# Three page buffers in paged attention, output weights loaded a stage earlier, and one-hop barriers in a two-layer decoder step

## The chip, the core and the metric

The kernel runs on one core of a Trainium2 chip. A core has five engines that run their own instruction streams: PE (matrix products), DVE and ACT (elementwise work), POOL (GpSimd) and SP (which here only issues transfers). Sixteen DMA engines move data between the main memory and the on-chip memory. The engines order their work by semaphores: one waits until a counter has reached a value, another adds to it.

The metric is the device time of one execution in microseconds; lower is better.

## What is computed

A prompt of 512 tokens and 8 samples of 8 new tokens each go through two layers. Layer 0 mixes tokens by softmax attention with a forget bias; the samples attend to 512 past rows each, which lie in four pages of 128 rows that a page table names. Layer 1 is an mLSTM. After each mixer comes a mixture of 32 experts, of which each token takes two.

```python
for layer in range(DEPTH):
    hp = rmsnorm(xp, norm_mix[layer]); hs = rmsnorm(xs, norm_mix[layer])
    if layer % N_MIXERS == 0:
        qp, kp, vp, lfp = fox_project(hp, fox_w_in[j], fox_b_f[j])
        cp = jnp.cumsum(lfp, axis=1)
        op = fox_attention(qp, kp, vp, cp, cp, 0)
        k_past = gather_pages(cache_k[j], page_table)
        v_past = gather_pages(cache_v[j], page_table)
        ...
        xp = xp + fox_output(op, fox_w_out[j])
        xs = xs + fox_output(os_, fox_w_out[j])
    else:
        ...
    # then x = x + hier_moe(rmsnorm(x)): top group, top 2 of its 8 experts,
    # each down(silu(x @ w_gate) * (x @ w_up)), weighted
```

## The kernel before

Everything is in 32-bit floats. The 576 tokens are five row tiles (four of 128 prompt rows, one of 64 sample rows). The program is seven phases: the projection of layer 0 (`fox_project`), its attention (`fox_attention`), its output product and experts (`out_and_experts(0, ...)`), the mLSTM projection, the mLSTM itself, `out_and_experts(1, ...)`, and the final norm with the outputs.
**Projection.** ACT squares each row tile, DVE scales it, PE turns it (L385), DVE puts it into `turned` with the gains (L495). Then PE makes the forget gates (L391) from all 576 tokens, and the keys in eight blocks of 128 columns (L357, `keys`). POOL meanwhile loads the past log-forget rows in a loop of 32 small transfers (L342), which starts when the last of the five square roots (L338) is done. From the fifth key block on PE turns these rows (L366, `turn_past`); it first waits for all 32 (`past_in`). Then come values (L416) and queries (L438). At its end SP fills the buffer `expert_rows` in main memory with nine transfers of 512 KB (`fill_rows`).

**Attention.** First the prompt: 8 pairs of heads, 4 query tiles each, `STEPS` = 32 steps. Per pair SP loads four blocks of forget rows (L235, `tri_rows`), and in the pairs' gaps a page each of sample 0's keys (SP) and values (POOL), both through `load_page` (L548). Then the samples b = 0 to 7, one after the other: PE turns the sample's four key pages (L714, `d_turn_keys`, in two halves), makes scores (L756), turns the weights of the sample before (L725, L726), multiplies them with its value pages (L738), and turns the result (L764). A sample has 2 MB of key pages and 2 MB of value pages. Key pages have two buffers, `kpg` and the memory of the prompt's queries; value pages have two, `vpg` and the memory of the prompt's keys. SP issues the keys of sample b once those of sample b-2 are turned (`kt_done`), POOL the values of b once those of b-2 are multiplied (`do_done`). Both second buffers are free only when the prompt's last scores are made (`s_done` at `STEPS`), so sample 1's pages are issued then.

**Output product and experts.** SP loads the 4 MB of output weights `w` into the memory of the third expert buffer (L1071). PE runs four products with no use (L191, `idle_products`), then the output product (L1175), which DVE adds to the residual rows `x` (`add_tile`). Then routing, and 16 pairs of experts, whose weights (6 MB a pair, L1039, L1047 and L1061) go round three buffers: the next pair's load is issued when PE has finished with the pair three before it. The loads of the third buffer wait for the whole output product.

## Time and profile before

| | us |
|---|---|
| median of 3 runs | 1433.36 |
| lowest and highest | 1431.96, 1446.88 |
| the profiled execution's own time | 1446.13 |
| its span in the trace | 1444.4 |

| engine | busy us | share |
|---|---|---|
| PE | 1258.4 | 87% |
| DVE | 370.4 | 26% |
| ACT | 246.7 | 17% |
| POOL | 214.1 | 15% |

The transfers move 342.60 MB, 237 GB/s over the span. Read these shares with care: they are means over phases that have different limits. For a change in one phase one reads that phase: which engine has gaps there, and what ended them. A matmul row gives the start, the busy time, the line, the tiles and in brackets the idle time ahead of it with what ended it. PEq, POOLq and SPq are the engines' own instruction queues.

### The profile page before, as it was taken

The fourth block names the chain that finished last, engine by engine and source line by source line (L and its number), as shares of the span: only waits on it lengthen the run. The fifth ranks groups of instructions, "written<-read, shape, count | busy, mean of one in ns | idle before, by whom it ended". The sixth has DMA issues, their size and how long they took to land.

```text
span 1444.4 us, 16231 instructions
## 1 busy us (share of the span) xinstructions
PE 1258.4 (87%) x6275; PEld 665.3 (46%) x6275; DVE 370.4 (26%) x792; ACT 246.7 (17%) x571; POOL 214.1 (15%) x268
## 2 busy tenths in 40 slices
PE   6999998889789989988877999999879989988780
PEld 4764575556544533333324764444654543333230
DVE  4131003554310541111115400112620441111115
ACT  2000004653210301000003200013420201000001
POOL 2300002321200011111101000211930011111102
PEclk9999999999989999999998999999979999999995
DMA  8310534749958579999959032212139469999975
GB/s 279 100 44 23 188 132 116 236 151 323 366 190 338 192 262 418 419 420 419 416 231 318 21 110 50 84 47 81 31 137 363 181 212 413 420 419 419 420 297 204
DMA packets 104397, 342.60 MB, mean 237 GB/s; under 512 B 21534, under 2 KB 40162, under 8 KB 80506
## 3 DMA queue, kind: packets, MB, share of 16 engines
q1 hardware_dynamic: 89176, 305.47, 55.5%
q0 software_dynamic: 14848, 35.94, 6.9%
q8 instruction: 54, 0.88, 0.3%
q14 instruction: 29, 0.24, 0.0%
q10 hardware_dynamic: 290, 0.07, 0.0%
HBM read 320.08 MB, written 36.02 MB: 247 GB/s over the span
## 4 chain that ended last, share of the span: by engine, by line
PE 55%; SPq 16%; DMA 12%; DVE 6%; issue 4%; ACT 2%; POOL 2%; POOLq 2%; DVEq 0%; ACTq 0%
SPq L1039 9%; PE ps L1759 8%; PE ps L1175 8%; PE ps L1250 7%; SPq L1061 4%; PE ps L438 4%; DMA moe_gu<-in_moe_w_up 4%; PE ps L416 4%; PE ps L1710 4%; DMA moe_wd<-in_moe_w_down 3%; PE ps L1268 2%; DMA fox_arena<-in_cache_k 2%; PE ps L357 2%; PE ps L696 1%; PE ps L1770 1%
## 5 line engine op out<-in xcount | busy, mean ns | idle before, releaser
L1250 PE MATMUL ps<-moe_gu,rows 128*64 128x512 f32 x1024 | 249.8, 644 | 49.9 <-DMA moe_gu<-in_moe_w_up 47.3
L1250 PEld LDWEIGHTS ps<-moe_gu,rows 128*64 128x64 f32 x1024 | 82.4, 148 | 197.6 <-issue 188.8
L1759 PE MATMUL ps<-mwblk,turned 128*128 128x512 f32 x256 | 111.5, 593 | 2.3 <-DVE vaug L1962 1.5
L1175 PE MATMUL ps<-moe_gu,turned 128*128 128x512 f32 x256 | 110.2, 592 | 0.0
L1537 DVE TENSOR_TENSOR turned<-turned,ps 128x256 f32<-128x256 f32 x32 | 13.5, 421 | 304.8 <-ACT turned L1353 304.8
L1135 POOL DMA_INDIRECT expert_rows<-turned,moe_row x32 | 32.0, 1001 | 390.8 <-ACT turned L1363 358.4
L1268 PE MATMUL ps<-moe_wd,moe_rowsel 128*64 128x512 f32 x352 | 80.4, 598 | 2.8 <-DMA moe_wd<-in_moe_w_down 2.8
L1175 PEld LDWEIGHTS ps<-moe_gu,turned 128*128 128x128 f32 x256 | 48.7, 190 | 61.5 <-issue 61.5
L1759 PEld LDWEIGHTS ps<-mwblk,turned 128*128 128x128 f32 x256 | 48.0, 190 | 61.0 <-issue 57.4
L1353 ACT ACTIVATE turned<-ps 128x256 f32<-128x256 f32 x32 | 12.3, 383 | 301.9 <-PE ps L1250 301.9
L357 PE MATMUL ps<-turned,fox_arena 128*128 128x288 f32 x256 | 63.1, 407 | 0.0
L438 PE MATMUL ps<-turned,fox_arena 128*128 128x288 f32 x256 | 62.3, 407 | 0.0
L416 PE MATMUL ps<-fox_arena,turned 128*128 128x512 f32 x128 | 57.6, 606 | 2.5 <-issue 2.5
L191 PE MATMUL ps<-cst 128*128 128x512 f32 x76 | 46.4, 756 | 13.1 <-POOLq L2506 13.1
L438 PEld LDWEIGHTS ps<-turned,fox_arena 128*128 128x128 f32 x256 | 48.6, 190 | 14.1 <-issue 0.8
L1710 PE MATMUL ps<-turned,mwblk 128*128 128x288 f32 x224 | 54.5, 406 | 0.0
L357 PEld LDWEIGHTS ps<-turned,fox_arena 128*128 128x128 f32 x256 | 48.3, 190 | 13.4 <-issue 0.5
L241 POOL TENSOR_TENSOR fox_arena<-fox_arena,cst 128x256 f32<-128x256 f32 x32 | 23.1, 727 | 205.8 <-DMA fox_arena<-negc_rows 205.6
L1710 PEld LDWEIGHTS ps<-turned,mwblk 128*128 128x128 f32 x224 | 42.6, 190 | 11.7
L873 DVE CUSTOM_DVE_ANT_0 fox_arena<-ps,fox_arena 128x128 f32<-128x128 f32 (+3 forms) x64 | 28.2, 478 | 66.4 <-PE ps L673 66.4
L1128 POOL DMA_INDIRECT turned<-h_rows,moe_row x32 | 33.2, 1036 | 76.6 <-DVE moe_row L1496 43.1
L1542 DVE COPY turned<-ps 128x512 f32<-128x512 f32 x32 | 22.1, 691 | 86.8 <-PE ps L1268 86.8
(345 smaller groups left out, 1522.7 us busy)
## 6 DMA issues: line engine op xcount, KB each, us to landing
moe_gu<-in_moe_w_gate SPq DMA_DIRECT2D x56, 1024.0 KB, 21.8
moe_gu<-in_moe_w_up SPq DMA_DIRECT2D x56, 1024.0 KB, 24.0
moe_wd<-in_moe_w_down SPq DMA_DIRECT2D x44, 1024.0 KB, 24.3
rows<-in_moe_w_down SPq DMA_DIRECT2D x20, 1024.0 KB, 22.3
fox_arena<-in_cache_k SPq DMA_DIRECT2D x32, 512.0 KB, 8.2
fox_arena<-in_cache_v POOLq DMA_DIRECT2D x32, 512.0 KB, 9.5
fox_arena<-in_fox_w_in SPq DMA_DIRECT2D x6, 2048.0 KB, 10.3
mwblk<-in_mlstm_w_in SPq DMA_DIRECT2D x6, 2048.0 KB, 8.6
```

What stands on the lines that cost most here:

```text
L191: pe.matmul(ps[:, bank, :], ident, const("ones")[:, 0:512], start=True, stop=True)
L357: mm = pe.matmul(ps[:, 2 * (g % 3) + half, 0:HT], wblk[:, g // 4, c, (g % 4) * P:(g % 4 + 1) * P], turned[:, c, half * HT:(half + 1) * HT] ...
L416: mm = pe.matmul(ps[:, m % 4, :], turned[:, c, n * P:(n + 1) * P], wblk[:, (2 + blk) % 3, c, :], start=(c == 0), stop=(c == KC - 1))
L438: mm = pe.matmul(ps[:, 2 * ((g + 2) % 4) + half, 0:HT], wblk[:, (4 + g // 4) % 3, c, (g % 4) * P:(g % 4 + 1) * P], turned[:, c, half * HT: ...
L1039: sp.dma_start(gu[p % SLOTS][:, half, k], i[name][layer, 2 * p + half].rearrange("(p c) n -> p c n", c=KC)).then_inc(gu_in[p % SLOTS], 16)
L1061: sp.dma_start(wd[p % SLOTS][:, half], i["moe_w_down"][layer, 2 * p + half].rearrange("(p c) n -> p c n", c=2)).then_inc(down_in[p % SLOTS ...
L1128: pool.indirect_dma_start(xg[:, s, :], None, h_dram[layer], bass.IndirectOffsetOnAxis(ap=rows_of(0, p), axis=0), bounds_check=TOK - 1, oob ...
L1175: mm = pe.matmul(ps[:, 2 * n + half, :], turned[:, c, n * P:(n + 1) * P], w[:, c, half * 512:half * 512 + 512], start=(c == 0), stop=(c == ...
L1250: mm = pe.matmul(ps[h, 2 + p % 2, :].rearrange("s (k f) -> s k f", k=2), xT[:, c, h], gu[s][:, half, :, c, :], start=(c == 0), stop=(c == ...
L1268: mm = pe.matmul(ps[h, 5 + n, :], aT[p % 2][:, m, h], wd[s][:, half, m, n * 512:(n + 1) * 512], start=(m == 0), stop=(m == 1))
L1710: mm = pe.matmul(ps[:, bank + half, 0:HT], wblk[:, k % 3, c, g * P:(g + 1) * P], turned[:, c, half * HT:(half + 1) * HT], start=(c == 0), ...
L1759: mm = pe.matmul(ps[:, m % 4, :], turned[:, c, n * P:(n + 1) * P], wblk[:, k % 3, c, :], start=(c == 0), stop=(c == KC - 1))
```

## The change

1. **Three buffers of pages.** The keys' third buffer is `x[:, 0:4, :]` (the residual rows of the prompt), the values' third is the memory of `sc`. SP loads sample 1's key pages into `x` during the last four pairs of the prompt, sample 2's after the prompt's scores, and from then on sample b+1's when sample b-2's are turned. POOL issues sample 1's values after the prompt's scores, sample 2's after its outputs, then b+1's when b-2's are multiplied. As `x` is overwritten, SP loads the four prompt row tiles again at the end of attention (`x_again`), and DVE waits for them ahead of the first `add_tile`.
2. **Output weights a phase earlier.** SP loads layer 0's output weights during the last samples, into memory that is then free; `multiply_out` of layer 0 no longer runs the four products of `idle_products`.
3. **Barriers.** Every engine, POOL too, drains, adds one to `together`, and waits for all five.
4. **First phase.** Nine products of the identity ahead of the first turning; an activation ahead of the first square; gates and first key block in two halves of 288 tokens, the first after three row tiles; three instead of four PSUM places for turned tiles.
5. The filling of `expert_rows` is gone.
6. Sample 0's first four key turnings stand ahead of the last pair's value product; DVE's first key copy waits for that product.

```diff
@@ -174,14 +174,9 @@
 
 
 
-        filled = lasting("filled")
-
-        def fill_rows(sp):
-
-            for row in range(0, 2 * TOK, P):
-                sp.dma_start(y_dram[row:row + P, :], x[:, 0, :]).then_inc(filled, 16)
-
         back_in = [[lasting(f"back_in{layer}_{n}") for n in range(NT)] for layer in range(2)]
+        w0_in, x_again = [lasting(f"w0_in{c}") for c in range(KC)], lasting("x_again")
+        W0_AT = 2 * 8 * D - SB * NPAGE
         back = []
...
             fox_project(pages, arena, qT, kT, v, tri)
-            fox_attention(part, qT, kT, v, pages)
+            w0 = arena[:, W0_AT:W0_AT + KC * D].rearrange("p (c d) -> p c d", d=D)
+            fox_attention(part, qT, kT, v, pages, w0)
             dx.close()
-            out_and_experts(0, i["fox_w_out"][0])
+            out_and_experts(0, i["fox_w_out"][0], w0)
...
-                fill_rows(sp)
                 sp.wait_ge(kv_out, 96)
-                sp.wait_ge(filled, 16 * (2 * TOK // P))
...
+            def flip(pe, n):
+
+                r = ROWS[n]
+                pe.wait_ge(scaled, n + 1)
+                if n >= 3:
+                    pe.wait_ge(gained, n - 2)
+                for c in range(KC):
+                    mm = pe.transpose(ps2[:, 1 + n % 3, c * P:c * P + r], rows[0:r, n, c:D:KC], ident[0:r, 0:r])
+                mm.then_inc(flipped, 1)
+
+            def gates_half(pe, half):
+
+                for c in range(KC):
+                    mm = pe.matmul(ps[0:FH, 6 + half, 0:HT], wf[:, c, :], turned[:, c, half * HT:(half + 1) * HT],
+                                   start=(c == 0), stop=(c == KC - 1))
+                if half:
+                    mm.then_inc(f_done, 1)
+
+            def first_half(pe, half):
+
+                for c in range(KC):
+                    mm = pe.matmul(ps[:, half, 0:HT], wblk[:, 0, c, 0:P], turned[:, c, half * HT:(half + 1) * HT],
+                                   start=(c == 0), stop=(c == KC - 1))
+                if half:
+                    mm.then_inc(k_done, 1)
...
             def pe_(pe):
                 pe.wait_ge(ident_in, 16)
-                for n, r in enumerate(ROWS):
-                    pe.wait_ge(scaled, n + 1)
-                    if n >= 4:
-                        pe.wait_ge(gained, n - 3)
-                    for c in range(KC):
-                        mm = pe.transpose(ps2[:, n % 4, c * P:c * P + r], rows[0:r, n, c:D:KC], ident[0:r, 0:r])
-                    mm.then_inc(flipped, 1)
+                for _ in range(9):
+                    pe.matmul(ps[:, 0, 0:P], ident, ident, start=True, stop=True)
+                for n in range(4):
+                    flip(pe, n)
                 pe.wait_ge(wf_in, 32)
+                pe.wait_ge(gained, 3)
+                gates_half(pe, 0)
+                flip(pe, L)
+                pe.wait_ge(w_in[0], 16)
+                first_half(pe, 0)
                 pe.wait_ge(gained, NT)
-                for c in range(KC):
-                    for half in range(2):
-                        mm = pe.matmul(ps[0:FH, 6 + half, 0:HT], wf[:, c, :], turned[:, c, half * HT:(half + 1) * HT],
-                                       start=(c == 0), stop=(c == KC - 1))
-                mm.then_inc(f_done, 1)
+                gates_half(pe, 1)
+                first_half(pe, 1)
                 for g in range(PAIRS):
-                    keys(pe, g)
+                    if g:
+                        keys(pe, g)
                     if g == 2:
...
-                act.wait_ge(zeroed, 1)
+                act.wait_ge(zeroed, 2)
+                act.activation(rstd[:, 0:1], ms[:, 0:1], ACT.Square)
...
+                dve.memset(ms[:], 1.0).then_inc(zeroed, 1)
...
-            kpg = [part("kpg"), part("qT", NPAGE * D)]
-            vpg = [part("vpg"), part("kT", NPAGE * D)]
-            kpg = [t.rearrange("p (g n) -> p g n", g=NPAGE) for t in kpg]
-            vpg = [t.rearrange("p (g n) -> p g n", g=NPAGE) for t in vpg]
+            kpg = [part("kpg").rearrange("p (g n) -> p g n", g=NPAGE), x[:, 0:NPAGE, :],
+                   part("qT", NPAGE * D).rearrange("p (g n) -> p g n", g=NPAGE)]
+            vpg = [t.rearrange("p (g n) -> p g n", g=NPAGE)
+                   for t in (part("vpg"), part("kT", NPAGE * D), part("sc", NPAGE * D))]
+            RING = len(kpg)
...
-            later = part("tri")
+            later = part("tri")[:, 6 * PROMPT:]
...
                         past_rows(p - 2 - NPAGE)
-                for b in range(1, SB):
-                    if b == 1:
-                        sp.wait_ge(s_done, STEPS)
-                        sp.wait_ge(dec_own, PREP)
-                    else:
+                    if p >= PAIRS - NPAGE:
+                        load_page(sp, i["cache_k"], kpg[1], pages, 1, p - PAIRS + NPAGE, k_in[1])
+
+                def keys_in(b):
+                    for g in range(NPAGE):
+                        load_page(sp, i["cache_k"], kpg[b % RING], pages, b, g, k_in[b % RING])
+
+                sp.wait_ge(s_done, STEPS)
+                sp.wait_ge(dec_own, PREP)
+                keys_in(2)
+                for b in range(2, SB):
+                    if b + 1 < SB:
                         sp.wait_ge(kt_done, PAIRS * (b - 1))
-                    for g in range(NPAGE):
-                        load_page(sp, i["cache_k"], kpg[b % 2], pages, b, g, k_in[b % 2])
-                    if b >= 2:
-                        past_rows(b)
+                        keys_in(b + 1)
+                    past_rows(b)
+
+                def w_chunk(c):
+                    sp.dma_start(w0[:, c, :], i["fox_w_out"][0][c * P:(c + 1) * P, :]).then_inc(w0_in[c], 16)
+
+                sp.wait_ge(kt_done, PAIRS * (SB - 1))
+                w_chunk(0)
+                w_chunk(1)
+                sp.wait_ge(do_done, SB - 1)
+                for c in range(2, 6):
+                    w_chunk(c)
+                sp.wait_ge(dtopped, SB)
+                w_chunk(6)
+                w_chunk(7)
+                sp.wait_ge(kt_done, PAIRS * SB)
+                for n in range(NT - 1):
+                    sp.dma_start(x[:, n, :], i["x_prompt"][0, n * P:(n + 1) * P, :]).then_inc(x_again, 16)
...
+                def values_in(b):
+                    for g in range(NPAGE):
+                        load_page(pool, i["cache_v"], vpg[b % RING], pages, b, g, v_in[b % RING])
...
                     if b == 1:
                         pool.wait_ge(s_done, STEPS)
-                    if b >= 2:
+                        values_in(1)
+                        pool.wait_ge(o_kept, PAIRS)
+                        values_in(2)
+                    if b >= 2 and b + 1 < SB:
                         pool.wait_ge(do_done, b - 1)
-                    for g in range(NPAGE if b else 0):
-                        load_page(pool, i["cache_v"], vpg[b % 2], pages, b, g, v_in[b % 2])
+                        values_in(b + 1)
...
+                    if s == STEPS + 1:
+                        pe.wait_ge(m_done, 2 * STEPS)
+                        pe.wait_ge(k_in[0], 64)
+                        d_turn_keys(pe, 0, range(0, 4))
                     if s >= 5 and s % QT_ == 1:
                         values(pe, (s - 5) // QT_)
                     if 1 <= s <= STEPS:
                         turn_weights(pe, s - 1)
-                pe.wait_ge(m_done, 2 * STEPS)
                 for b in range(SB + 1):
-                    if b < SB:
-                        pe.wait_ge(k_in[b % 2], 64 * (b // 2 + 1))
+                    if 0 < b < SB:
+                        pe.wait_ge(k_in[b % RING], 64 * (b // RING + 1))
                         d_turn_keys(pe, b, range(0, 4))
...
                     if b and p == 1:
                         dve.wait_ge(ds_done, b)
+                    elif p == 1:
+                        dve.wait_ge(pv_done, PAIRS)
...
-            w_in = [sem(tag + f"w_in{c}") for c in range(KC)]
+            w_in = [sem(tag + f"w_in{c}") for c in range(KC)] if layer else w0_in
...
-                for c in range(KC):
+                for c in range(KC if layer else 0):
                     sp.dma_start(w[:, c, :], w_dram[c * P:(c + 1) * P, :]).then_inc(w_in[c], 16)
...
-                idle_products(pe, 4, 0)
+                if layer:
+                    idle_products(pe, 4, 0)
...
+                if layer == 0:
+                    dve.wait_ge(x_again, 16 * (NT - 1))
...
-                if who == "pool":
-                    eng.wait_ge(together, 4 * (n + 1))
-                    eng.drain().then_inc(cleared, 1)
-                else:
-                    eng.drain().then_inc(together, 1)
-                    if who == "sp" and "late" in phase:
-                        phase["late"](eng)
-                    eng.wait_ge(cleared, n + 1)
-                    alone(eng)
+                eng.drain().then_inc(together, 1)
+                if who == "sp" and "late" in phase:
+                    phase["late"](eng)
+                eng.wait_ge(together, 5 * (n + 1))
+                alone(eng)
```

PE's order at the start of the program: L385 and (after) L362 turn row tiles, L391 and L368 are the gates, L357, L376 and L351 the keys, L401 the identity products. Before:

```order
L385 MATMUL ps<-cst,rows 128x128 x32
L385 MATMUL ps<-cst,rows 128x64 x8
L391 MATMUL ps<-turned,fox_arena 16x288 x16
L357 MATMUL ps<-turned,fox_arena 128x288 x48
L399 MATMUL ps<-cst,fox_arena 128x16 x4
```

After:

```order
L401 MATMUL ps<-cst 128x128 x9
L362 MATMUL ps<-cst,rows 128x128 x32
L368 MATMUL ps<-turned,fox_arena 16x288 x8
L362 MATMUL ps<-cst,rows 128x64 x8
L376 MATMUL ps<-turned,fox_arena 128x288 x8
L368 MATMUL ps<-turned,fox_arena 16x288 x8
L376 MATMUL ps<-turned,fox_arena 128x288 x8
L351 MATMUL ps<-turned,fox_arena 128x288 x32
```

Half of the gates and half of the first key block moved ahead of the rest, and the small tile's turning between them; nothing is left out, nine products are added.

PE's order where the prompt's attention ends and the samples begin: L685 and L737 turn the last weights, L696 and L748 multiply values, L703 and L755 spread the sums, L714 and L766 turn sample 0's keys. Before:

```order
L685 MATMUL ps<-cst,fox_arena 128x128 x18
L696 MATMUL ps<-rows,fox_arena 64x512 x2
L696 MATMUL ps<-rows,fox_arena 64x384 x2
L696 MATMUL ps<-rows,fox_arena 64x256 x2
L696 MATMUL ps<-rows,fox_arena 64x128 x2
L703 MATMUL ps<-cst,pa_inv 64x128 x8
L714 MATMUL ps<-cst,fox_arena 128x128 x32
```

After:

```order
L737 MATMUL ps<-cst,fox_arena 128x128 x18
L766 MATMUL ps<-cst,fox_arena 128x128 x16
L748 MATMUL ps<-rows,fox_arena 64x512 x2
L748 MATMUL ps<-rows,fox_arena 64x384 x2
L748 MATMUL ps<-rows,fox_arena 64x256 x2
L748 MATMUL ps<-rows,fox_arena 64x128 x2
L755 MATMUL ps<-cst,pa_inv 64x128 x8
L766 MATMUL ps<-cst,fox_arena 128x128 x16
```

Sixteen of the 32 key turnings moved ahead of the value product.

SP's order at the end of attention; the last rows of each belong to the next phase. L548 and L570 load key pages, L607 and L631 forget rows of the samples, L1071 and L659 the output weights. Before:

```order
L548 DMA fox_arena<-in_cache_k 128x1024
L607 DMA fox_arena<-negs_rows 128x1x512
L1071 DMA moe_gu<-in_fox_w_out 128x1024 x8
L1073 DMA moe_wr<-in_moe_w_group 128x8x4
L1074 DMA moe_wr<-in_moe_w_router 128x8x32
```

After:

```order
L570 DMA x<-in_cache_k 128x1024
L631 DMA fox_arena<-negs_rows 128x1x512 x2
L659 DMA fox_arena<-in_fox_w_out 128x1024 x8
L672 DMA x<-in_x_prompt 128x1024 x4
L1130 DMA moe_wr<-in_moe_w_group 128x8x4
L1131 DMA moe_wr<-in_moe_w_router 128x8x32
```

Twelve transfers of 512 KB now stand in SP's queue ahead of the barrier, where none stood: the eight of the weights, which came behind it, and four new ones.

## Rows read from the trace of the kernel before

**Rows 1.** The windows by phase: time, busy per engine, granted clock, DMA share, GB/s

```profile
233.00:317.00 84.00, 71.90 (x512) 42.21 (x513) 46.10 (x175) 54.36 (x168) 29.38 (x44) 0.97 0.60 182
317.00:347.00 30.00, 28.85 (x320) 19.81 (x321) 12.94 (x28) 9.81 (x19) 3.40 (x7) 0.94 0.88 308
356.00:373.00 17.00, 12.85 (x156) 7.89 (x146) 6.32 (x16) 3.42 (x7) 5.04 (x10) 0.90 1.03 363
415.00:424.00 9.00, 6.42 (x9) 2.75 (x10) 0.15 (x2) 0.00 (x0) 0.56 (x2) 0.62 0.60 215
424.00:479.00 55.00, 55.00 (x130) 24.16 (x130) 3.97 (x6) 3.51 (x6) 1.10 (x2) 1.00 0.69 273
521.00:704.00 183.00, 161.75 (x726) 62.71 (x722) 29.69 (x38) 15.83 (x38) 23.81 (x24) 0.94 1.00 409
```

**Rows 2.** PE's timeline over the samples: start, busy, line, tiles, idle before

```profile
328.75 1.97 PE L714 MATMUL ps<-cst,fox_arena 128*128 128x128 f32 x16
337.80 1.91 PE L714 MATMUL ps<-cst,fox_arena 128*128 128x128 f32 x16
...
346.80 1.91 PE L714 MATMUL ps<-cst,fox_arena 128*128 128x128 f32 x16
...
353.43 3.46 PE L738 MATMUL ps<-fox_arena 128*32 128x256 f32 x40 [2.07 <-DMA fox_arena<-in_cache_v]
```

**Rows 3.** The same timeline, the later samples and the phase's end

```profile
373.14 3.68 PE L714 MATMUL ps<-cst,fox_arena 128*128 128x128 f32 x16 [4.16 <-DMA fox_arena<-in_cache_k]
...
377.68 2.29 PE L714 MATMUL ps<-cst,fox_arena 128*128 128x128 f32 x16
...
397.00 1.97 PE L714 MATMUL ps<-cst,fox_arena 128*128 128x128 f32 x16 [1.74 <-DMA fox_arena<-in_cache_k]
...
401.54 2.37 PE L738 MATMUL ps<-fox_arena 128*32 128x256 f32 x40
...
409.08 4.05 PE L738 MATMUL ps<-fox_arena 128*32 128x256 f32 x40 [0.69 <-ACT fox_arena L846]
```

**Rows 4.** The transfers' issues between 300 and 420: count, size, time to landing

```profile
fox_arena<-in_cache_k SPq DMA_DIRECT2D x28, 512.0 KB, 10.1
fox_arena<-in_cache_v POOLq DMA_DIRECT2D x28, 512.0 KB, 9.8
...
fox_arena<-negs_rows SPq DMA_DIRECT2D x6, 256.0 KB, 14.3
```

**Rows 5.** The chain that ended last, at the first two barriers: start, us, what

```profile
229.24 0.65 ACT fox_arena L476
...
230.01 2.69 POOLq L2506
```

**Rows 6.** The same chain at the second barrier

```profile
414.22 0.22 DVE turned L936
...
414.77 2.67 POOLq L2506
```

**Rows 7.** The drains of POOL at the barriers: least, median, most, ns

```profile
L2506 POOLq DRAIN  x7: 34/2663/2686, 230.0 to 1443.9; - x7
```

**Rows 8.** PE's timeline at the start of the output product

```profile
417.58 6.26 PE L191 MATMUL ps<-cst 128*128 128x512 f32 x8 [3.41 <-POOLq L2506]
423.69 1.88 PE L1175 MATMUL ps<-moe_gu,turned 128*128 128x512 f32 x4
```

**Rows 9.** The timeline of the first phase's start, all engines

```profile
5.24 1.28 ACT L465 ACT_TABLE_LOAD   x1 [5.24 <-DMA x<-in_x_prompt]
...
15.13 0.15 DVE L485 TENSOR_SCALAR ms<-sq 128x1 f32<-128x1 f32 x1
15.19 1.22 DVE L495 TENSOR_TENSOR turned<-ps,gains 128x1024 f32<-128x1024 f32 x1
...
19.08 9.61 PE L391 MATMUL ps<-turned,fox_arena 128*16 128x288 f32 x32 [0.88 <-DVE turned L495]
...
64.40 0.54 POOL L342 DMA_DIRECT2D fox_arena<-in_cache_logf  x1 [0.98 <-issue]
...
69.36 1.04 PE L366 MATMUL ps<-cst,fox_arena 128*16 128x128 f32 x8 [1.09 <-DMA fox_arena<-in_cache_logf]
```

**Rows 10.** SP's queue at the start of the output phase, first and last issues

```profile
417.54 3.85 SPq L1071 DMA_DIRECT2D moe_gu<-in_fox_w_out  x8
...
422.08 4.26 SPq L1074 DMA_DIRECT2D moe_wr<-in_moe_w_router  x1
...
430.67 0.42 SPq L1039 DMA_DIRECT2D moe_gu<-in_moe_w_gate  x1
...
435.83 1.98 SPq L1061 DMA_DIRECT2D moe_wd<-in_moe_w_down  x2
```

**Rows 11.** Forget rows of the prompt (L235): issue to landing, least, median, most

```profile
DMA to landing us min/median/max: 3.5/4.9/8.6
```

19 lines of the change are left out of this document (10 added, 9 removed).

## The prediction

> **What bounds the kernel now.** I read the windows by phase first [rows 1]. In the expert stage (521 to 704) the DMA share is 1.00 at 409 GB/s: the weights are the limit, and PE waits for them. But this stream is started by PE (each load waits for PE to have finished with a buffer), so if all before it comes earlier, the stage does too. Over the prompt's attention (233 to 317) PE is busy 71.9 of 84 us and the DMA share is 0.60; in the samples (317 on) the share is 0.88 and then 1.03, so the pages are the limit there. Then PE's timeline over the samples: sample 1's first key turning begins at 328.75, sample 2's at 337.80, sample 3's at 346.80, without a wait: about 9.0 us each [rows 2]. Sample 7's begins at 397.00, after waits of 2.07, 4.16 and 1.74 us for pages among others [rows 2, 3]. Six periods took 68.25 us where six of 9.0 are 54.0. Last the chain of waits at the barriers: the last engine of the first phase ends at 229.9 and POOL's drain then takes 2.69 us [rows 5]; at the second, 2.67 us [rows 6].
>
> **Samples with three buffers.** The most it can give is 68.25 - 54.0 = 14.25 us. Is there bandwidth for it? After the prompt's scores (312) the kernel before moves 28 key and 28 value pages [rows 4]. After the change four key pages have come earlier, so 24 + 28 = 52 pages of 0.524 MB are left, 27.3 MB, and six forget rows of 0.26 MB: 28.8 MB. Saturated, this stage moved 363 GB/s (356 to 373) and the experts' 409 [rows 1]; I take 385: 75 us, plus some 2 us of gap because the third value buffer is free only at 322, so the last value page lands at about 389. Without waits sample 7 begins at 328.75 + 54.0 = 382.75, and its value product stands as far behind that as before, 409.08 - 397.00 = 12.1 us [rows 3]: 394.8. That fits. Its keys are tighter. They are issued when sample 4's are turned, about 360, and what stands ahead of them is all but five to eight of the pages: 25 MB, landing at 312 + 65 + 2 = 379 at 385 GB/s, at 383 at 363. So sample 7 waits between nothing and a few us. I take 1.25 us off: **13.0 us**; bounds 9 (363 GB/s, and the output weights in between) and 14.25. Sample 0 itself gains nothing: the key turnings fill 0.8 us of PE's idle time ahead of the last value product, but DVE's copies still start behind that product.
>
> What hides the rest: four more key pages in the last four pairs of the prompt, one a pair, 1.3 us of DMA each at 400 GB/s. Forget rows land in 4.9 us at the median, 8.6 at most [rows 11], and are issued one pair ahead, 84 / 8 = 10.5 us. Some 5 us of slack cover 1.3. Cost: 0. The filling of `expert_rows`, 4.7 MB, lies under the query products of the first phase, whose chain is PE's; its going gives 0. The residual rows (2 MB) come back by about 405 and are wanted at the first `add_tile`, some 50 us later: 0.
>
> **Barriers.** POOL's drain took 2.66 us at the median of seven, 34 ns at least [rows 7]. It is long in the phases in which POOL has issued transfers, short in the other two of the middle. After the change POOL drains when its own work is done. At the first two barriers POOL is done long before (its last row turning's load in the first phase is issued at 64.40 [rows 9]), so the drain is hidden. 2.69 + 2.67, less 0.1 us each for the signal: **5.2 us**, and 0.3 us for a PE that stands still 1 us and not 3.6 ahead of the prompt's first scores. At the third and sixth barrier POOL's scatter is what ends last, so its drain stays, and the next phase's first work waits for transfers issued ahead of it: 0. The fourth and fifth lose one signal each: **0.2 us**.
>
> **Output product.** The four idle products run from 417.58 to 423.69, 6.11 us [rows 8]; they go, as the weights are there. 
>
> **First phase.** The table load of ACT (1.28 us at 5.24) goes ahead of the first row tile's arrival [rows 9], and the first turnings run warm, so DVE's chain is 1.3 us earlier and gets back 0.5 us of waiting: the last mean (15.13) about 1.8 us earlier, the third `keep` (15.19 + 1.22) too. Half the gates start at about 14.7, not 19.08, and without their slow start (9.61 us, where 32 records of this size take 7.85 at the upper clock). PE gains 4.4 + 1.8 = some 6 us of lead. But at the fifth key block it waits for the 32 past rows, 1.09 us even before, until 69.36 [rows 9]. POOL's loop of issues is what decides that, and it starts only 1.8 us earlier, so this point comes at 67.5. PE now stands still there for some 4 to 5 us. After an idle time of 4.16 us the same turnings took 3.68 + 2.29 us at 373, against 1.97 + 1.91 elsewhere [rows 2, 3]: 2.1 us, and 0.6 on those between. So the 1.8 us are paid back. **0 us**; bounds -1 and +1.8. The nine identity products end about when the first tile is scaled.
>
> **The sum.** 13.0 + 5.2 + 0.3 + 0.2 + 3.4 + 0 = 22.1 us. The profiled execution took 1446.13 us, its span 1444.4; it would take 1424.0. It stands 12.8 above the median of the runs, 1433.36; I take the same difference from that: **1411.3**. With all lower bounds (9, 3, -1 us) it is 16.7 us: 1416.7; with all upper ones (14.25, 6.11, 1.8) 27.9: 1405.5.
>
> **Rivals.**
> *The pages stay the limit.* A third buffer adds no bandwidth. If the transfers run at 363 GB/s, as between 356 and 373, and not faster, the samples need 79 us, sample 7 waits 4 to 5 us and PE's clock falls again: the term is 8 to 9, the time 1415.5. For it: the share is 1.03 already [rows 1]. Against it: the rate over saturated stretches reaches 409, and the last keys have over 20 us from issue to use. The Trainium skill ("DMA: Bandwidth & Descriptors", "Issuing engines are not separate DMA queues") states that transfers of all engines share the same 16 DMA engines; the keys on SP and the values on POOL then slow one another, as the 14.3 us landing of a 256 KB row [rows 4] shows. Chance 0.20.
> *SP comes late to the barrier.* Twelve transfers stand ahead of its drain. If the queue held no more than some eight, its last issue would wait and the second barrier come 4 us late: 1415. For it: one issue behind the weights took 4.26 us. Against it: from 430.67 SP issued twelve of 1 MB in 7 us [rows 10]. Chance 0.06.
> *The forget rows come late.* The added pages stand ahead of the next pair's rows in SP's queue. It decides from the point where a row takes over 10.5 us less the mask, that is twice its median landing. From there each us goes straight into the last four pairs. At 2 to 4 us a pair 8 to 16 us are lost and the time is within 1% of before (1419 to 1427): chance 0.11. At the price of a whole landing more a pair, 8.6 us, 34 us are lost and it is 1446, slower than before; this needs rows at 17 us. Chance 0.03. Against both: the pairs 2 to 5 carry the same kind of page today and keep their period.
>
> **Chances and range.** Forecast 0.60 (1405 to 1417), pages 0.20, SP 0.06, rows 0.14. A measurement of this kernel can tell about 1%, 14.3 us, from no change: faster means under 1419. Nearly all of the first three is faster; the rows' cases are not, and the runs of before spread over 15 us, which could cost the verdict. Faster 0.84, same 0.12, slower 0.04. Range 1403 to 1420.
>
> **What would show it.** The first gates start near 14.7, but the turning of past rows near 67.5 after a wait of 4 us or more. The prompt's attention starts within 0.5 us of ACT's last copy. Pairs keep 10.4 us. Samples 1 to 7 start 9.0 us apart, the last near 380 on the new time axis (about 3 us less than here); a wait of some us on key pages ahead of sample 6 or 7 is the first rival. The output product starts within 0.5 us of attention's end and runs its first 4 us or so at 1.2 GHz. The expert stage takes what it took, only earlier. I am wrong if the weights' stream gives time back, if pairs 4 to 7 lengthen, or if SP's drain ends behind DVE's.

## The result and the profile after

Three comparisons of the changed kernel were made, each beside runs of the kernel before. The first is the one the prediction is measured by; the two others were made later, with more runs. Experiments were made on different chips, so they are compared by their ratio to the kernel before.

| comparison | changed, us (median, lowest to highest) | before, us (median) | ratio and 95% interval |
|---|---|---|---|
| first | 1423.15 (1417.14 to 1428.57, 4 runs) | 1436.47 | 0.9889 [0.9852, 0.9925] |
| second | 1417.81 (1416.92 to 1421.56, 5 runs) | 1438.82 | 0.9862 [0.9842, 0.9882] |
| third | 1421.01 (1416.40 to 1426.12, 6 runs) | 1439.32 | 0.9876 [0.9841, 0.9912] |
| forecast | 1411.3 (1403 to 1420) | 1433.36 | 0.9846, worked out |

The kernel is faster by 1.1% to 1.4%, on average of the three ratios by 1.24%, 17.9 us of 1438. The forecast was 22.1 us. The direction was right and the median of the first comparison lies 3 us above the range. Of the 11.8 us between 1411.3 and 1423.15 some are of the base: 1433.36 was the median of three runs, and in the later comparisons the kernel before took 1437.9 to 1441.25. In the first comparison the gain was 13.3 us, 8.8 less than forecast; over all three it was 17.9, 4 us less, and behind it stand terms that were off in both directions by more than that.

The profiled execution of the changed kernel took 1428.57 us (span 1426.7, before 1444.4), the longest of its four; that of the kernel before, 1446.13 us, was long for its kernel too. Four places of its trace tell most. First PE's timeline over the later samples, the rows that answer to [rows 2, 3]: start, busy, line, tiles, and in brackets the idle time before and its releaser. L766 turns keys, L777 turns the softmax's weights, L790 is the value product.

```profile
348.75 1.91 PE L766 MATMUL ps<-cst,x 128*128 128x128 f32 x16
...
359.12 1.97 PE L766 MATMUL ps<-cst,fox_arena 128*128 128x128 f32 x16 [1.22 <-DMA fox_arena<-in_cache_k]
363.23 0.66 PE L777 MATMUL ps<-cst,fox_arena 128*128 128x128 f32 x4 [2.14 <-ACT fox_arena L894]
...
372.86 1.97 PE L766 MATMUL ps<-cst,fox_arena 128*128 128x128 f32 x16 [2.51 <-DMA fox_arena<-in_cache_k]
376.92 0.66 PE L777 MATMUL ps<-cst,fox_arena 128*128 128x128 f32 x4 [2.10 <-ACT fox_arena L894]
...
386.87 1.97 PE L766 MATMUL ps<-cst,x 128*128 128x128 f32 x16 [2.83 <-DMA x<-in_cache_k]
391.21 0.66 PE L777 MATMUL ps<-cst,fox_arena 128*128 128x128 f32 x4 [2.38 <-ACT fox_arena L894]
...
402.83 3.83 PE L790 MATMUL ps<-fox_arena 128*32 128x256 f32 x40 [0.69 <-ACT fox_arena L901]
407.27 0.44 PE L816 MATMUL ps<-cst,fox_arena 128*128 128x128 f32 x2 [0.62 <-DVE fox_arena L985]
408.42 1.96 PE L1233 MATMUL ps<-fox_arena,turned 128*128 128x512 f32 x4 [0.70 <-DVEq L2564]
```

Sample 1 begins at 321.71 and samples 1 to 4 stand 9.0 us apart, but samples 5, 6 and 7 wait for key pages, and each then waits a second time in L777, for a softmax whose maximum waited for the forget row. Sample 7 begins 65.2 us behind sample 1; the forecast was 68.25 - 13.0 = 55.25, in the kernel before it was 68.25. And the last value product stands 81.1 us behind sample 1, against 80.3 before: in this profile the stage gained nothing.

Second, the maximum's wait for the forget rows in the same samples, and the rows' time from issue to landing in us (14.3 at the median before [rows 4]):

```profile
L631 SPq DMA_DIRECT2D fox_arena<-negs_rows x6: 535/564/721, 323.2 to 376.0; - x6
...
  DVE fox_arena L967: 19.2, 3
...
DMA to landing us min/median/max: 11.2/18.0/27.0
```

Third, what the DMA queues carried between the first page issue and sample 7's start (q1 is SP's with keys and rows, q0 POOL's with values: packets, MB, share):

```profile
DMA packets 8250, 28.72 MB, mean 354 GB/s; under 512 B 899, under 2 KB 899, under 8 KB 8240
...
q1 hardware_dynamic: 4308, 14.23, 50.1%
q0 software_dynamic: 3932, 14.35, 49.1%
```

All keys and rows that sample 7 needs are 24 pages and six rows, 14.2 MB, and q1 has just carried them. But q0 has carried as much, nearly all 14.7 MB of the values, and the last 2.1 MB of those are wanted only 16 us later. The transfers were busy throughout, partly with bytes that weren't due. How the two queues share the engines shows best where both have work all the time, here from 372 to 382:

```profile
q0 software_dynamic: 544, 1.99, 53.6%
q1 hardware_dynamic: 544, 1.85, 49.5%
```

The packets are equal, the bytes are not. In the three stretches of 10 us before this one the counts are 538 and 539, 527 and 526, 536 and 535; two more profiles of the same kernel differ by 21 packets at most in these stretches. Before 342, with one queue or the other out of work at times, they are not equal. A forget row of 256 KB is 144 packets, as many as a page of 512 KB: where they have a queue of their own, below, six rows are 864 packets and five pages 720.

Fourth, the start of the prompt's attention, behind the barrier of [rows 5]. Before, PE stood idle for 3.65 us, and the value products of the first pair (L696) began 11.35 us behind the scores:

```profile
232.84 3.05 PE L673 MATMUL ps<-fox_arena 64*128 64x128 f32 x12 [3.65 <-POOLq L2506]
...
244.19 2.38 PE L696 MATMUL ps<-rows,fox_arena 128*64 128x512 f32 x16
```

After, the idle time is 0.87 us, and they (L748) begin 9.29 us behind the scores:

```profile
228.69 0.93 PE L725 MATMUL ps<-fox_arena 64*128 64x128 f32 x8 [0.87 <-ACTq L2564]
...
237.98 2.38 PE L748 MATMUL ps<-rows,fox_arena 128*64 128x512 f32 x16
```

In the windows (granted clock third from the end) this stretch has a clock of 1.00; the second row is the output product, which ran at the full clock from its first record and took 55.2 us:

```profile
228.60:238.00 9.40, 7.92 (x50) 4.30 (x50) 5.93 (x26) 8.14 (x25) 2.77 (x4) 1.00 0.64 201
...
408.40:463.60 55.20, 55.18 (x130) 24.31 (x132) 3.95 (x7) 3.30 (x6) 1.45 (x4) 1.00 0.67 267
```

The same stretch in the kernel before had 0.75:

```profile
232.80:244.20 11.40, 10.12 (x50) 5.11 (x50) 5.91 (x26) 8.48 (x25) 3.37 (x5) 0.75 0.82 189
```

The output product begins 1.15 us behind the start of the attention's last product, 408.42 - 407.27. Before, the last product began at 413.74, and the output product 9.95 us behind it, at 423.69 [rows 8]:

```profile
413.74 0.44 PE L764 MATMUL ps<-cst,fox_arena 128*128 128x128 f32 x2 [0.61 <-DVE fox_arena L928]
```

In the changed kernel the clock is back at 1.00 between the last value product and the output product. In the kernel before it had come back too (0.82 in the mean: 1.00 until 415.5, 0.50 from 416.5 on), and it fell again while PE stood idle for 3.41 us at the barrier:

```profile
406.70:408.40 1.70, 0.44 (x2) 0.21 (x3) 0.93 (x3) 0.00 (x0) 0.00 (x0) 1.00 1.03 424
```

```profile
413.20:417.50 4.30, 0.44 (x2) 0.20 (x2) 0.93 (x3) 0.00 (x0) 0.00 (x0) 0.82 0.00 0
417.50:423.70 6.20, 6.12 (x9) 2.58 (x10) 0.15 (x2) 0.00 (x0) 0.56 (x2) 0.57 0.83 293
```

Everything behind the output product came earlier by what had been gained until there (the last phase ends 17.7 us earlier).

### The profile page after: what moved, and what is told of

Its sections match the earlier page's. It is cut to its first block, busy times and chain, and to the rows that moved or that the text cites. A ratio compares the mean times of both kernels' runs of the same rounds, so it can differ in the third digit from the quotient of the medians.

```text
span 1426.7 us, 16246 instructions
## 1 busy us (share of the span) xinstructions
PE 1237.4 (87%) x6285; PEld 654.8 (46%) x6285; DVE 370.4 (26%) x793; ACT 246.7 (17%) x572; POOL 214.4 (15%) x268
## 4 chain that ended last, share of the span: by engine, by line
PE 54%; SPq 16%; DMA 12%; DVE 7%; issue 4%; POOL 3%; ACT 2%; POOLq 2%; DVEq 0%; ACTq 0%
SPq L1096 10%; PE ps L1819 8%; PE ps L1233 8%; PE ps L1308 7%; PE ps L458 4%; DMA moe_gu<-in_moe_w_up 4%; SPq L1118 4%; PE ps L436 4%; PE ps L1770 4%; DMA fox_arena<-negs_rows 3%; PE ps L1326 3%; PE ps L351 2%; DMA moe_wd<-in_moe_w_down 1%; PE ps L748 1%; PE ps L1830 1%
## 5 line engine op out<-in xcount | busy, mean ns | idle before, releaser
L1308 PE MATMUL ps<-moe_gu,rows 128*64 128x512 f32 x1024 | 243.6, 630 | 57.1 <-DMA moe_gu<-in_moe_w_up 53.8
L458 PE MATMUL ps<-turned,fox_arena 128*128 128x288 f32 x256 | 62.3, 406 | 0.0
L436 PE MATMUL ps<-fox_arena,turned 128*128 128x512 f32 x128 | 59.0, 619 | 2.9 <-issue 2.9
L1233 PE MATMUL ps<-fox_arena,turned 128*128 128x512 f32 x128 | 55.2, 593 | 0.7 <-DVEq L2564 0.7
L351 PE MATMUL ps<-turned,fox_arena 128*128 128x288 f32 x224 | 55.2, 406 | 0.0
L1233 PE MATMUL ps<-moe_gu,turned 128*128 128x512 f32 x128 | 55.2, 593 | 0.0
L458 PEld LDWEIGHTS ps<-turned,fox_arena 128*128 128x128 f32 x256 | 48.6, 190 | 14.1 <-issue 0.8
L186 PE MATMUL ps<-cst 128*128 128x512 f32 x68 | 40.0, 731 | 9.5 <-POOLq L2564 8.3
L1770 PEld LDWEIGHTS ps<-turned,mwblk 128*128 128x128 f32 x224 | 42.6, 190 | 11.8
L351 PEld LDWEIGHTS ps<-turned,fox_arena 128*128 128x128 f32 x224 | 42.2, 190 | 11.4
L1600 DVE COPY turned<-ps 128x512 f32<-128x512 f32 x32 | 22.1, 691 | 88.0 <-PE ps L1326 88.0
```

The costliest lines, as they stand in the source:

```text
L186: pe.matmul(ps[:, bank, :], ident, const("ones")[:, 0:512], start=True, stop=True)
L351: mm = pe.matmul(ps[:, 2 * (g % 3) + half, 0:HT], wblk[:, g // 4, c, (g % 4) * P:(g % 4 + 1) * P], turned[:, c, half * HT:(half + 1) * HT] ...
L436: mm = pe.matmul(ps[:, m % 4, :], turned[:, c, n * P:(n + 1) * P], wblk[:, (2 + blk) % 3, c, :], start=(c == 0), stop=(c == KC - 1))
L458: mm = pe.matmul(ps[:, 2 * ((g + 2) % 4) + half, 0:HT], wblk[:, (4 + g // 4) % 3, c, (g % 4) * P:(g % 4 + 1) * P], turned[:, c, half * HT: ...
L1233: mm = pe.matmul(ps[:, 2 * n + half, :], turned[:, c, n * P:(n + 1) * P], w[:, c, half * 512:half * 512 + 512], start=(c == 0), stop=(c == ...
L1308: mm = pe.matmul(ps[h, 2 + p % 2, :].rearrange("s (k f) -> s k f", k=2), xT[:, c, h], gu[s][:, half, :, c, :], start=(c == 0), stop=(c == ...
```

## The experiments

Theory: the third buffer's bytes are there, but they land in the wrong order, since SP's queue (keys, rows) and POOL's queue (values) advance alike. The rival is that the bytes alone are the limit, which no order mends. A second question was how much the barriers gave.

To compare the samples in different profiles I use one interval: from POOL's first value page to the first record of the output phase on PE. It doesn't depend on when the attention began. Where the old barrier stands in it, its 2.7 us are taken off. It is called the **stage** below: 102.3 us before (312.54 to 417.58, less 2.7) and 102.1 in the changed kernel's first profile (306.32 to 408.42).

**Two buffers instead of three**, the rest as changed: from sample 2 on a sample's pages are sent for when those of the sample two before have been read.

```diff
-            kpg = [part("kpg")..., x[:, 0:NPAGE, :], part("qT", NPAGE * D)...]
-            vpg = [... (part("vpg"), part("kT", NPAGE * D), part("sc", NPAGE * D))]
+            kpg = [part("kpg")..., x[:, 0:NPAGE, :]]
+            vpg = [... (part("vpg"), part("kT", NPAGE * D))]
```

> The changed kernel with two buffers of pages in place of three: keys and values of a sample are sent for when the sample before last has been read, as before the change; all else of the change stays. Theory A (the order of landing: keys with rows on SP's queue and values on the software queue are served alike, so values land 12 to 17 us early and what is needed first lands last; the third buffer brought nothing): within 2 us of the changed kernel's profile (the last value product of the samples at 405 to 409 us, the changed kernel has 407.3). Rival B (the third buffer did pay, and something else of the change lost what was expected): 8 to 13 us longer, the last value product at 415 to 420 us.

Measured: 1426.45 us, 0.9908 [0.9878, 0.9938], stage 102.8. As the theory had it: no difference to the first comparison of the changed kernel, 0.9889, that could be told. The 407.3 in the expectation is the start of the attention's last product; it begins at 406.4 here, and the last value product at 403.4, in the changed kernel at 402.8. This was not the last word (below).

**The forget rows by ScalarE.** SP's loop no longer calls `past_rows(b)`; ACT issues them behind its exponentials:

```diff
                     act.activation(pr[:, b % 2, :], ..., ACT.Exp, ...).then_inc(dp_ready, 1)
+                    if b + 2 < SB:
+                        act.dma_start(dbias[:, b % 2, 0:PAST], negs_dram[:, b + 2, :]...).then_inc(db_in[b % 2], 16)
```

> The changed kernel with the forget rows of samples 2 to 7 sent for by ScalarE's own queue, right behind the exponentials of the sample two before, in place of standing behind four key pages on SP's queue. Theory A: the three waits of the maximum's turn (2.14, 2.10 and 2.38 us of TensorE's idle time at samples 2 to 5, with DVE waiting 5.4 to 7.2 us for the rows) go; the waits for key pages (1.22, 2.51, 2.83 us) stay or grow, since the bytes are the same; 2 to 6 us shorter. Rival B (the rows only share the wait with the pages: the bytes are the limit): the key waits grow by what the row waits lose, under 1 us. Rival C: rows land no sooner on the other queue, no change at all in the waits.

Measured: 1414.45 us, 0.9829 [0.9774, 0.9885], stage 93.6. The time is 6.7 us under the changed kernel's mean ratio of 0.9876, more than expected, with an interval of 8 us on either side. The rows land in 8.3 us, nobody waits for them, and of the key waits one is left. In PE's timeline (L765 turns keys, L789 is the value product):

```profile
358.30 1.91 PE L765 MATMUL ps<-cst,fox_arena 128*128 128x128 f32 x16
...
367.30 1.91 PE L765 MATMUL ps<-cst,fox_arena 128*128 128x128 f32 x16
...
378.11 1.97 PE L765 MATMUL ps<-cst,x 128*128 128x128 f32 x16 [1.66 <-DMA x<-in_cache_k]
...
390.20 4.05 PE L789 MATMUL ps<-fox_arena 128*32 128x256 f32 x40 [0.69 <-ACT fox_arena L903]
```

Sample 7 begins 76.2 us behind the first page issue of 301.9, 4.8 less than the 81.1 of the changed kernel. The key waits did not grow; that part of the expectation was wrong, and the queues say why. This is the same kernel, profiled again, from its first page issue to just past sample 7's start:

```profile
q1 hardware_dynamic: 3617, 13.20, 46.5%
q0 software_dynamic: 3358, 12.26, 43.6%
q10 hardware_dynamic: 864, 1.57, 6.5%
```

The rows' 1.57 MB travel on q10. When SP's queue is through with the keys, POOL's has carried 12.26 MB and not 14.35. Sample 7 can begin 2 MB earlier, 5 to 6 us at 354 GB/s. By packets, 864 of the 4320 that sample 7 needs have left SP's queue.

**The values by SP**, on one queue with keys and rows in order of need (`keys_in(b + 1)`, `past_rows(b)`, then the four value pages of b + 1).

> The changed kernel with the value pages of samples 1 to 7 issued by SP, on the same queue as keys and rows, in the order of need: keys of b+1, rows of b, values of b+1. Theory A (two queues served alike bring values 12 to 17 us too early): the waits at samples 4 to 7 shrink, sample 7 begins at 379 to 381 us in place of 386.9, and the kernel is 5 to 8 us shorter than the changed one. Rival B (the bytes by then are the limit, or one queue moves less than two): sample 7 begins at 385 us or later, within 2 us of the changed kernel or longer.

Measured: 1418.30 us, 0.9847 [0.9792, 0.9901], stage 96.6 (from SP's first page issue). Against the changed kernel's mean ratio this is 4 us shorter, which lies within its interval, and the wait for keys at sample 5 is gone. That fits an order that matters, but doesn't show it by itself: sample 7 begins at 384.4, some 4 us later than expected and near the rival's 385. SP waits for a product here before it may issue the next pages, and from the first issue to sample 7 the mean rate was 340 GB/s against 354.

**Half of the value pages.** This kernel leaves out two of each sample's four value pages and multiplies the other two twice, so its result isn't the reference's.

```diff
-                    for g in range(NPAGE):
+                    for g in range(2):
                         load_page(pool, i["cache_v"], vpg[b % RING], ...)
-                        src = vpg[b % RING][:, k, :] if k < NPAGE else ...
+                        src = vpg[b % RING][:, k % 2, :] if k < NPAGE else ...
```

> The changed kernel with two value pages per sample loaded in place of four (the value product reads the two twice, so this part of the computation isn't the reference's): 7.3 MB fewer over the samples' stage, all instructions of the engines the same. If transfers are what holds the samples apart, all six waits go, samples are 9.0 us apart from the first to the last (sample 7 begins 54 to 55 us after sample 1, 65.2 in the changed kernel) and the kernel is 9 to 12 us shorter. If something else holds them (SP's issue, the rows' chain), sample 7 begins 60 us or more after sample 1 and the kernel is under 5 us shorter.

Measured: 1410.33 us, 0.979 [0.9735, 0.9844], stage 90.1. Samples stand 9.0 us apart from the first to the last, sample 7 54.0 us behind sample 1, no wait for pages left. This is what the stage takes when no page is late: the changed kernel's stage is 12 us above it in its first profile, the one with ScalarE's rows 3.5 us.

**The barriers alone**, put into the kernel before (the change's last hunk and nothing else).

> The kernel before with the new barriers alone (every engine signals and waits for five signals). Theory: POOL's drain (2.67 us behind its software transfers) then runs beside the others' drains in place of behind them; the first two barriers give 2.6 us each and the later ones, whose drain is 0.03 us, under 0.2 us: 5.2 us shorter, 0.9964 of before, and a barrier's wait of 0.9 us in place of 3.65 ahead of the prompt's first scores. The prompt's first pair, 11.35 us in the kernel before with a clock of 0.75, then starts warm and gives 2 us more. Rival: POOL's drain ends last anyway, no gain.

Measured: 1425.78 us, 0.9927 [0.9907, 0.9946]: 10.5 us, twice what was forecast. PE's timeline (L191 are the idle products, L1175 is the output product):

```profile
227.77 0.93 PE L673 MATMUL ps<-fox_arena 64*128 64x128 f32 x8 [0.87 <-ACTq L2504]
...
237.06 2.38 PE L696 MATMUL ps<-rows,fox_arena 128*64 128x512 f32 x16
...
410.46 3.67 PE L191 MATMUL ps<-cst 128*128 128x512 f32 x8 [0.70 <-DVEq L2504]
414.27 55.20 PE L1175 MATMUL ps<-moe_gu,turned 128*128 128x512 f32 x128
```

I read four differences against the profile before: the wait at the first barrier 0.87 and not 3.65 (2.8), the prompt's first pair 9.29 and not 11.35 us (2.1), the second wait 0.70 and not 3.41 (2.7), the idle products 3.81 and not 6.11 us from their start to the next product (2.3) [rows 8]. Together 9.9. The barrier's wait was paid twice: PE stood still for 3.65 and 3.41 us, and part of what followed ran at the lower level (0.75 over the first pair, 0.57 over the idle products). Behind 0.87 and 0.70 us of idle time both have 1.00.

**Two buffers and ScalarE's rows**: the first two experiments together.

> Two buffers of pages (as in the first experiment) and the forget rows sent for by ScalarE (as in the second), the rest as changed. The last value product of the samples begins at 390.2 us with three buffers and ScalarE's rows, at 402.8 with three and SP's rows, at 403.4 with two and SP's rows. Theory A (both are needed: the third buffer's bytes are worth what was forecast, once the rows no longer stand behind four pages): the last value product begins 5 to 12 us later than with three buffers and ScalarE's rows, at 395 to 402 us. Rival B (the late rows were all, and the third buffer is worth nothing): at 389 to 393 us, the kernel as short as with three.

Measured: 1426.54 us, 0.9928 [0.9904, 0.9952], stage 102.0, last value product at 401.0: theory A. The rows' place is worth nothing that can be told without the third buffer, which with it is worth 8 to 9 us (102.0 against 93.6). One thing doesn't fit: this kernel has all of the change but the third buffer, and on the same chip it takes no less than the kernel before with the barriers alone (1425.78), though the output product's part should be in it.

**The rows ahead of the keys**, both on SP's queue (`past_rows(b)` moved ahead of the wait for `kt_done` and `keys_in(b + 1)`).

> The changed kernel with the forget rows of sample b still on SP's queue, but ahead of the four key pages of sample b+1 in place of behind them (issued from about 323, 332, ... us on). Theory A (what costs is that rows stand behind 2.1 MB of pages): rows land in 5 to 12 us in place of 18, before they are wanted, no wait of the maximum for them; the last value product begins within 3 us of that with ScalarE's rows (390.2). Rival B (a queue of its own is what helps, since queues are served alike): the rows are in time but the keys land late, the last value product at 396 to 403 us.

Measured: 1428.83 us, 0.9928 [0.9905, 0.9951], stage 106.9, last value product at 406.5: the worst of all with three buffers. The rows take 14.7 us at the median and nobody waits for them, but four waits for key pages add up to 10.4 us. SP's queue shows what was lost. `past_rows(2)` waits for a maximum, so key pages of sample 3, which the changed kernel issues at once behind those of sample 2, left only at 327.5:

```profile
304.79 4.30 SPq L570 DMA_DIRECT2D fox_arena<-in_cache_k  x4
326.14 0.56 SPq L631 DMA_DIRECT2D fox_arena<-negs_rows  x1
327.46 3.67 SPq L570 DMA_DIRECT2D fox_arena<-in_cache_k  x4
```

Rows in time and keys late is rival B's picture, but later than its 396 to 403 us, and the late issue would do the same. So this run did not separate its theories; it shows instead what an order on a queue costs when its head waits.

**The idle products kept.**

```diff
-                if layer:
-                    idle_products(pe, 4, 0)
+                idle_products(pe, 4, 0)
```

> The changed kernel with the four idle products ahead of the first output product kept. The prediction held that leaving them out costs 2.7 us of clock at the start of the output product. Theory A (TensorE goes from the samples' last products into the output product at 1.00 of clock, nothing is lost cold): 3.5 us longer at full clock (four products of 512 columns in f32, 0.87 us each), 6.1 us if they run at half the clock, and the output product no shorter than 55.17 us less 0.3. Rival B (it does run cold without them): the product 2 to 3 us shorter, the kernel 0.5 to 4 us longer.

Measured: 1424.25 us, 0.9902 [0.9864, 0.9940], against 0.9876 of the changed kernel in the mean: some 3.7 us longer, with intervals that overlap. The trace shows theory A: the idle products took 404.72 to 408.22, 3.5 us, and the output product 55.10 us.

**The old barriers in the changed kernel.**

> The changed kernel with the barriers of the kernel before, all else changed. The new barriers alone gave 10.5 us (7.8 to 13.4) against the forecast 5.2. Theory A (a barrier costs twice: its own 2.7 us of serial drain, and a TensorE clock of half that follows the idle 3.4 to 3.7 us, 2.1 us in the prompt's first pair and 2 to 3 us in what follows the second barrier): 8 to 11 us longer than the changed kernel, the output product's first 6 us at a clock under 0.9 and the product 57 to 58 us in place of 55.2. Rival B (only the drains): 5.2 us longer, the product still 55.2 us.

Measured: 1428.61 us, 0.9916 [0.9885, 0.9948]: 5.7 us above the changed kernel's mean (1.3 to 10.4 by this run's interval), less than the 8 to 11 expected. By the time alone that is rival B's number. The trace has theory A's pieces, though:

```profile
228.24 3.06 PE L725 MATMUL ps<-fox_arena 64*128 64x128 f32 x12 [3.65 <-POOLq L2566]
...
239.89 2.37 PE L748 MATMUL ps<-rows,fox_arena 128*64 128x512 f32 x16
...
406.03 58.13 PE L1233 MATMUL ps<-fox_arena,turned 128*128 128x512 f32 x128 [3.40 <-POOLq L2566]
```

Its window of 6 us at the start of the output product:

```profile
406.00:412.00 6.00, 5.97 (x7) 2.53 (x8) 0.15 (x2) 0.00 (x0) 0.55 (x2) 0.50 0.93 280
```

The waits of 3.65 and 3.40 are back, the first pair takes 11.65 us, and the output product 58.13 us, 3.0 more, with a clock of 0.50 in its first 6 us. These make 10.8 us. The stage was shorter here (95.1 us), which gave part of it back in this profile; whether that is chance or a consequence of the later start stays open, and with it what the barriers are worth in the changed kernel.

**The fourth key page by ScalarE**, from sample 3 on; the rows stay on SP's queue.

```diff
-                    for g in range(NPAGE):
+                    for g in range(NPAGE if b == 2 else NPAGE - 1):
                         load_page(sp, i["cache_k"], kpg[b % RING], pages, b, g, k_in[b % RING])
...
                     if b < SB:
                         d_keep_keys(b, 0)
+                    if 1 <= b < SB - 2:
+                        load_page(act, i["cache_k"], kpg[(b + 2) % RING], pages, b + 2, NPAGE - 1, k_in[(b + 2) % RING])
```

> The changed kernel with the last key page of samples 3 to 7 issued by ScalarE's queue (2.6 MB), the forget rows still on SP's queue, now behind three pages. Theory A (queues with work are served alike, and sample 7 begins when SP's queue has carried all its keys and rows; the other queue has carried as much by then): SP's queue carries 11.6 MB in place of 14.2, sample 7 begins 4 to 9 us earlier after the first page issue than the 81.1 us of the changed kernel, at 72 to 77 us, with less than 28 MB moved by then (28.7 in the changed kernel). Rival B (it is the lateness of the rows alone, by its waits in the maximum): sample 7 begins 79 us or more after the first page issue.

Measured: 1416.08 us, 0.9837 [0.9820, 0.9853], stage 93.3: theory A, 0.7 us outside its span of 72 to 77. No wait for pages is left; sample 7 begins at 382.46, 77.7 us behind the first issue, with 26.84 MB carried. Transfers no longer set this time: all samples stand 9.0 to 9.9 us apart. Most stand 9.6 apart and not 9.0, because ACT issues the page ahead of its exponentials, for which PE then waits in L777. ACT's timeline, and then the queues up to sample 7's start:

```profile
335.77 0.60 ACT L890 ACTIVATE rows<-ps 128x512 f32<-128x512 f32 x1 [4.78 <-PE ps L766]
336.45 0.35 ACTq L570 DMA_DIRECT2D x<-in_cache_k  x1
336.85 0.77 ACT L894 ACTIVATE fox_arena<-fox_arena,dnegtop 128x576 f32<-128x576 f32 x1 [0.48 <-issue]
```

```profile
q0 software_dynamic: 3441, 12.56, 44.9%
q1 hardware_dynamic: 3590, 11.53, 41.6%
q10 hardware_dynamic: 720, 2.62, 9.3%
```

No single queue has more than 12.6 MB here. ScalarE's has 720 packets for 2.62 MB, against 864 for the rows' 1.57 MB: in packets the two repairs move about as much.

**The old first phase in the changed kernel** (order of the gates, table load and idle products as before).

> The changed kernel with the first phase's order of the kernel before (no idle products ahead of the turning, no early table load, all gates behind all tokens). By the profiles the first phase ends 1.4 us earlier in the changed kernel (227.8 against 229.2), while its end lay between 223.9 and 227.8 in six profiles of this same code, by how much of it ran at half the clock. Theory A: 1 to 3 us longer, the past rows turned from about 69 us on in place of 66, a cold restart of the clock there. Rival B: no difference that can be measured, under 1 us.

Measured: 1427.25 us, 0.9896 [0.9868, 0.9925]: 2.9 us above the mean of the changed kernel, inside the uncertainty. The prompt's scores begin at 230.5 here.

**The changed kernel, both repairs, and two buffers again.** The intervals above overlap, so the changed kernel was run again on one chip beside the one with two buffers, and on another beside the two repairs.

> The changed kernel as it is, on one chip beside the kernel with two buffers, to tell what the third buffer alone is worth. From the first page issue to the start of the output product (less 2.7 us where the old barrier stood between, less 3.7 us of idle products where they stood) the profiles with three buffers and rows on SP's queue gave 102.6, 100.3, 98.1 and 95.6 us, those with two 103.3 and 102. Theory A: three buffers are worth 2 to 6 us in the mean, and the first profile of the changed kernel was an unlucky one: this profile at 95 to 101 us, the median 1420 to 1424 us. Rival B: nothing at all, 101 to 104 us and the same median as with two.

> The changed kernel with two buffers of pages, as in the first experiment, beside the changed kernel on the same chip. Theory A: 2 to 6 us longer than it. Rival B: the same within 1.5 us.

Measured: changed kernel 1417.81 us, 0.9862 [0.9842, 0.9882], stage 96.8; two buffers 1426.20 us, 0.9918 [0.9899, 0.9938], stage 104.5. 8.4 us apart: the third buffer does pay, more than expected here, and my reading of the first profile (nothing gained) was a reading of its most unlucky one. Its waits are of the same kind in this profile, only fewer: DVE waited 10.6 us for rows, not 19.2.

> The changed kernel with both the forget rows and the fourth key page of samples 3 to 7 on ScalarE's queue. Each alone took away all or all but one of the waits for pages (samples 9.0 to 9.6 us apart). Theory A (with the order of landing right the samples are bound by TensorE's own chain of 9.0 us): no wait left, from the first sample with its keys early to the output product 73 to 74 us as with either alone, and the time within 3 us of theirs (1414.5 and 1416.1). Rival B (they add up): 3 us or more shorter than the better of the two.

Measured: 1419.24 us, 0.9862 [0.9839, 0.9885], stage 94.0. No gain over either alone: neither theory, and on this chip no less than the changed kernel as it is (1417.81), though its stage is 2.8 us shorter than in that one's profile. There is a new wait, for the value pages that now are the ones to come late (landing 16.3 us at the median, 11.8 with the page alone on ScalarE):

```profile
377.94 4.00 PE L789 MATMUL ps<-fox_arena 128*32 128x256 f32 x40 [3.27 <-DMA fox_arena<-in_cache_v]
```

That fits the same rule from its other side: ScalarE's queue has both rows and pages to carry now, and the values' queue gets less. Why the time is not shorter stays open.

> The forget rows on ScalarE's queue, as in the second experiment, on one chip beside the changed kernel. From the first page issue to the output product the three kernels with rows or a page on ScalarE's queue took 94.1, 93.8 and 94.5 us, the five profiles with all of them on SP's queue 102.6, 100.3, 98.1, 97.3 and 95.6 (mean 98.8). Theory A: the order of landing is worth the difference, 4 to 5 us in the time, 94 to 95 us in this profile. Rival B: under 1.5 us, the first comparison was luck of the runs.

> The fourth key page of samples 3 to 7 on ScalarE's queue, on the same chip. Theory A: 4 to 5 us shorter than the changed kernel, 93 to 95 us from the first page issue to the output product, with no wait for pages. Rival B: under 1.5 us shorter.

> The changed kernel as it is, beside these two on the same chip: 96 to 103 us from the first page issue to the output product, 0.986 to 0.989 of the kernel before.

Measured on one chip: rows by ScalarE 1415.58 us, 0.9838 [0.9804, 0.9873], stage 93.1; page by ScalarE 1414.29 us, 0.9829 [0.9796, 0.9863], stage 93.3; changed kernel 1421.01 us, 0.9876 [0.9841, 0.9912], stage 98.2. The repairs are 5.4 and 6.7 us shorter than the changed kernel: theory A. Of five or six runs each, two of the changed kernel (1416.40 and 1417.43) are shorter than the longest of each repair.

The stage by scheme of loading:

| buffers, and who sends for rows and keys | stage, us | mean |
|---|---|---|
| two, SP (before, barriers alone, first and again) | 102.3, 105.1, 102.8, 104.5 | 103.7 |
| three, SP (changed x3, idle kept, old barriers, old first phase) | 102.1, 96.8, 98.2, 99.8, 95.1, 97.5 | 98.3 |
| three, rows or a page by ScalarE (five profiles) | 93.6, 93.1, 93.3, 93.3, 94.0 | 93.5 |
| half of the value pages | 90.1 | 90.1 |
| three, all by SP; two, rows by ScalarE; three, rows first | 96.6, 102.0, 106.9 | |

## Why the prediction was right in sign and short in size

**Samples with three buffers: forecast 13.0, measured 5.4 as changed (the stage's means; 8.4 on the chip that ran both); 10.2 with the rows or a page on another queue.** This is the step that failed. Its bytes were right (28.8 MB; 28.72 had been carried when sample 7 began) and its ceiling of 14.25 us too (the half-value kernel is 13.6 under the two-buffer mean). Wrong was "what stands ahead of them is all but five to eight of the pages": next to nothing stood behind sample 7's keys. Of the last 2.1 MB of values, which were not due, all but 0.3 MB had landed before them. I had counted bytes in the order of need, but two queues with work are served alike, so POOL's landed the values of samples 5 to 7 12 to 17 us early in this profile, while SP's, with the rows on top of the keys, was the one that everybody waited for. The Trainium skill ("DMA: Bandwidth & Descriptors", "Queues, rings and completion order") states it: each DMA engine takes turns between the queues that have work for it. By that rule two queues that both have work get turns alike, and the trace agrees, 544 packets and 544 from 372 to 382. Wrong by a second piece was the rate: 385 GB/s assumed between 363 and 409, 354 measured. For the 26.7 MB that sample 7 really needs that is 6 us. In this profile the 1.8 to 2 MB out of order are 5 us more, and the late row of sample 7 with the lower clock behind it 3.9 (last value product 16.0 us behind the sample's start, not 12.1).

The rival "the pages stay the limit" named the right place, nearly the right rate (363 GB/s) and 8 to 9 us for this term; with it the time would have been 1415.5. It deserved more than 0.20. Its reason was the bytes alone, though, and the kernels with rows or a page on ScalarE's queue move the same bytes in a shorter stage. Nor did the 14.3 us of a row show what it took them for: the row stood behind four pages in its own queue, and on ScalarE's it landed in 8.3. "The forget rows come late" was meant for the pairs of the prompt, where nothing happened, while in the samples the same queue made the rows late.

**Barriers: forecast 5.2 + 0.3, measured 10.5 (7.8 to 13.4).** The drains were sized right: 2.8 and 2.7 us. Mis-sized was the clock behind them. The prompt's first pair gained 2.1 us, not 0.3, and what follows the second barrier 2.3 us that were not in the sum at all. Both are read in the kernel before; with the old barriers put back into the changed kernel the whole was 5.7 us, so 10.5 is not sure to carry over.

**Output product: forecast 3.4, measured 3.5, by luck.** I took the idle products at 6.11 us and 2.7 us of lost clock from them. The step "so now the output product itself begins at 1.2 GHz" failed: it ran at 1.00 from its start. Behind the new barrier they would take 3.5 to 3.8 us and there is no loss. The 2.7 us were about right for a barrier that keeps PE idle 3.4 us: with the old one the product took 3.0 us longer. Two edits were costed each against the kernel before, and they share the same clock. The Trainium skill ("TensorE: Matmul & The Clock Gate", "What's actually happening") has throttling as the state without activity. By that rule an idle time as short as the new barrier's need not cost the clock, and the trace agrees (1.00 from the product's first record), even though the last value product ahead of the barrier had begun at the lower level. I had read that level as lasting until the barrier; in the windows above it doesn't, in either kernel.

**First phase: forecast 0 (-1 to +1.8), measured nothing that can be told.** The gates begin at 15.66, not 14.7; the past rows are turned from 66.11, earlier than the 67.5 forecast, behind a wait of 1.62 us and not of 4 or more. Over 16 profiles with the new first phase the prompt's scores begin at 226.8 in the mean (224.7 to 229.1), over three with the old one at 229.4, the old barrier's 2.8 us taken off. At sample 1's start the same profiles stand at 323.1 and 323.4 (the first pair's 2.1 us taken off as well where the old barrier stands), so next to nothing of these 2.6 us gets that far (below).

**What held:** pairs kept their 10.4 us, no wait for the residual rows shows ahead of the first `add_tile`, SP was not late at the second barrier, the experts' stretch moved 407 GB/s where it moved 409. What the filling of `expert_rows` was worth no run tells by itself. By the experiments the sum is 10.5 + 3.5 + 5.4 = 19.4 us, with 5.7 for the barriers 14.6, and 17.9 were measured.

## What to carry to other kernels

Where transfers are the limit, count what each queue must carry up to the moment of need, not all bytes together, and count it in packets: queues with work advanced alike here, so the queue that carries more of what is due first sets the time, and a small transfer moved to an idle queue can be worth as much as a buffer. Read a barrier's cost with what follows it: an idle time of PE of 3.4 to 3.65 us was paid again in clock here, and an edit that shortens it changes the price of every edit behind it. And one profile is one draw: for a stage that transfers bound, this one varied by 7 us between profiles of one scheme.

## What had not been expected of the hardware

- POOL's drain takes 2.66 to 2.69 us in the four phases in which it had issued transfers and 0.03 to 0.05 in the three others [rows 7]; what it cost the kernel before was about 5 us at each of the first two barriers, not 2.7.
- An earlier start of the prompt's attention was given back. From the prompt's first scores to sample 1 it is 97.2 to 97.6 us in the five profiles with the new first phase and barriers that start it before 226, and 93.0 to 93.1 in the three that start it behind 228.6; those between have 95.8 to 97.5. In the profile that starts at 228.69 the clock is 1.00 between 300 and 320 us; in the one that starts at 224.73 it is 0.80. Sample 1 begins at 321.71 in the one and 322.27 in the other. The window of the changed kernel:

```profile
300.00:320.00 20.00, 15.03 (x128) 10.13 (x128) 9.31 (x26) 8.70 (x22) 3.46 (x7) 1.00 0.62 223
```

  And that of the kernel with ScalarE's rows:

```profile
300.00:320.00 20.00, 15.03 (x99) 10.52 (x101) 8.28 (x20) 7.57 (x18) 4.36 (x8) 0.80 0.71 257
```

  PE was not idle more in the second (15.03 us busy in both). What lowers the clock there is open.
- Issuing from another engine is more than a saving of issue time: rows of 256 KB landed in 8.3 us on ScalarE's queue and in 18.0 on SP's (14.8 in a second profile), at the same total of bytes.
